# The head of a decoder layer on one Trainium2 core: halved first loads, products ahead of the token sums, ten idle products

## The reference

```
xn   = rms_norm(h) * g
proj = xn @ w_in        # query/key-value latents, rope key, recurrence input and gate, branch gates
attn = MLA(...)         # 8 heads, latent attention, causal
rec  = RG-LRU(...)      # causal conv of 4, gates a and i, linear recurrence, gelu gate
                        # a = exp(-8 * sigmoid(...) * softplus(-rg_lambda))
h = h + (sigmoid(g_a) * attn + sigmoid(g_r) * rec) @ w_out
h = h + MoE(rms_norm(h))   # 32 experts, top 4 of each token, clamped SwiGLU
out = rms_norm(h)[meta tokens dropped]
```

## Time and profile before

| | |
|---|---|
| median of 3 runs | 1166.68 us (1165.93 to 1167.15) |
| profiled execution, its own time | 1166.7 us |
| its span | 1164.9 us |
| TensorE busy | 1130.6 us (97%) |
| VectorE, ScalarE busy | 229.1 us, 189.3 us |
| granted TensorE clock, mean | 0.996 |
| HBM read | 440.53 MB |

### The profile page before, as it was taken

How to read it: one execution, slowest core, us unless ns; L and a number is a source line. 1 busy time by engine, 2 the same in 40 slices (tenths; PEclk the granted TensorE clock), 3 DMA queues, 4 the chain that set the end, 5 groups by cost and what they waited for, 6 DMA issues and landing times.

```text
span 1164.9 us, 13326 instructions
## 1 busy us (share of the span) xinstructions
PE 1130.6 (97%) x5608; PEld 524.5 (45%) x5608; DVE 229.1 (20%) x538; ACT 189.3 (16%) x412; POOL 0.2 (0%) x4
## 2 busy tenths in 40 slices
PE   8999999999999999999999999999999989999987
PEld 7778888844333333434343333333333333333422
DVE  5557510223011111111111111111111111111112
ACT  2466610022011010101011110101010101010102
POOL 0000000000000000000000000000000000000000
PEclk9999999999999999999999999999999999999999
DMA  9944436558999999999999999999999999999996
GB/s 374 396 152 174 159 150 248 224 203 333 416 431 430 430 428 437 433 430 433 432 433 432 432 433 432 433 432 434 432 432 433 433 433 433 432 426 428 430 425 271
DMA packets 30598, 442.14 MB, mean 380 GB/s; under 512 B 4640, under 2 KB 5152, under 8 KB 8160
## 3 DMA queue, kind: packets, MB, share of 16 engines
q1 hardware_dynamic: 27792, 438.93, 89.3%
q10 hardware_dynamic: 2768, 2.67, 0.7%
HBM read 440.53 MB, written 1.05 MB: 379 GB/s over the span
## 4 chain that ended last, share of the span: by engine, by line
PE 85%; DMA 13%; ACT 1%; another core or an unknown queue 0%; issue 0%; DVE 0%; SPq 0%; DVEq 0%; ACTq 0%
PE ps L941 33%; PE ps L960 16%; PE ps L577 11%; DMA work<-in_w_exp_dram 8%; PE ps L928 5%; PE ps L916 5%; DMA ring<-in_w_exp_dram 4%; PE ps L798 2%; PE ps L865 2%; PE ps L887 2%; PE ps L822 1%; ACT work L1405 1%; PE ps L950 1%; PE ps L922 1%; PE ps L661 1%; PE ps L614 1%
## 5 line engine op out<-in xcount | busy, mean ns | idle before, releaser
L941 PE MATMUL ps<-ring,work 128*64 128x512 f32 x1536 | 344.3, 600 | 11.7 <-DMA ring<-in_w_exp_dram 11.7
L941 PEld LDWEIGHTS ps<-ring,work 128*64 128x64 f32 x1536 | 109.9, 138 | 230.3 <-issue 219.0
L1857 DVE TENSOR_SCALAR work<-ps 128x512 f32<-128x512 f32 x32 | 22.1, 692 | 724.9 <-PE ps L941 724.9
L577 PE MATMUL ps<-work,ring 128*128 128x256 f32 (+1 forms) x560 | 125.9, 384 | 0.0
L941 PE MATMUL ps<-work 128*64 128x512 f32 x512 | 115.8, 596 | 1.9 <-DMA work<-in_w_exp_dram 1.9
L960 PE MATMUL ps<-ring,work 128*64 128x512 f32 x512 | 113.8, 596 | 3.9 <-ACT work L1405 3.8
L960 PE MATMUL ps<-work 128*64 128x512 f32 x504 | 112.5, 596 | 4.4 <-ACT work L1405 3.8
L577 PEld LDWEIGHTS ps<-work,ring 128*128 128x128 f32 x560 | 105.4, 190 | 17.1 <-issue 0.9
L941 PEld LDWEIGHTS ps<-work 128*64 128x64 f32 x512 | 35.3, 137 | 77.8 <-issue 73.6
L960 PEld LDWEIGHTS ps<-ring,work 128*64 128x64 f32 x512 | 35.3, 137 | 71.9 <-issue 63.0
L928 PE MATMUL ps<-work 64*128 64x512 f32 x256 | 67.5, 627 | 0.0
(11 more groups left out here) (261 smaller groups left out, 612.8 us busy)
## 6 DMA issues: line engine op xcount, KB each, us to landing
ring<-in_w_exp_dram SPq DMA_DIRECT2D x40, 4096.0 KB, 42.2
work<-in_w_exp_dram SPq DMA_DIRECT2D x20, 4096.0 KB, 42.1
ring<-in_w_exp_dram SPq DMA_DIRECT2D x38, 2048.0 KB, 18.3
work<-in_w_exp_dram SPq DMA_DIRECT2D x19, 2048.0 KB, 17.3
ring<-in_w_mix_dram SPq DMA_DIRECT2D x29, 1024.0 KB, 7.4
ring<-in_w_exp_dram SPq DMA_DIRECT2D x20, 1024.0 KB, 7.7
work<-in_w_exp_dram SPq DMA_DIRECT2D x9, 1024.0 KB, 11.9
ring<-in_w_mix_dram SPq DMA_DIRECT2D x2, 576.0 KB, 18.5
```

The source lines that it names most:

```text
L577: ins = nc.tensor.matmul(ps[part:part + width, b, 0:hi - lo], wv[:, k, o:o + width], rows[:, k, lo:hi], start=(k == 0), stop=(k == KT - 1))
L941: ins = nc.tensor.matmul(ps[CAP * c:CAP * c + CAP, b, :], xeT[:, k, CAP * (u % 2):CAP * (u % 2) + CAP], wu[:, k % SPAN, 512 * q:512 * q + ...
L1857: V.tensor_scalar(hg, ps[:, 0, :], LIMIT, None, ALU.min).then_inc(glu_ready, 1)
```

## The change

SyncE issues `vec` (all the small vectors, 101 floats a partition) first and then slot 0 in two halves, which are its blocks 0 to 3 and 4 to 7, each with a semaphore of its own (`head_in`); the later loads follow unchanged. ScalarE issues x in two halves instead of two quarters; SyncE issues none of x. All four squares are at ScalarE. The first products begin with the first halves; the token sums stand in front of block 6; the long idle product is gone, and there are ten short ones for nine. On VectorE the first two softplus instructions go ahead of `xw`, the long chain behind the squares of `cq`. On ScalarE the Exp comes first and the Sqrt table is loaded behind the squares.

```diff
-MIX_LANDINGS = [len(range(s, M0, SLOTS)) for s in range(SLOTS)]
+MIX_LANDINGS = [len(range(s, M0, SLOTS)) - (s == 0) for s in range(SLOTS)]
...
-            for c in (0, 2):
-                spe.dma_start(xT[:, 2 * c:2 * c + 2, :], xT_in[:, 2 * c:2 * c + 2, :]).then_inc(xT_in_s[c], 16)
             spe.dma_start(vec[:, :], vec_in[:, :]).then_inc(vec_in_s, 16)
+            for c in range(2):
+                q = SLOT // 2
+                spe.dma_start(ring[:, 0, q * c:q * c + q], w_mix[0, :, q * c:q * c + q]).then_inc(head_in[c], 16)
             for n, (kind, a, w) in enumerate(LOADS):
                 s = n % SLOTS
+                if n == 0:
+                    continue
...
-            keep_clock(0, 9)
+            keep_clock(0, 10)
...
-            keep_clock_long(2, xsq[:, 0, :], 1)
-            wait_load(load_at[("in", 0)])
+            def token_sums():
+                for k in range(KT):
+                    if k % 2 == 0:
+                        pe.wait_ge(xsq_act, k // 2 + 1)
...
             wv = wslot(load_at[("in", 0)], KT)
             for k in range(KT):
+                if k == 6:
+                    token_sums()
+                if k % 4 == 0:
+                    pe.wait_ge(head_in[k // 4], 16)
                 pe.wait_ge(xw_ready, k + 1)
...
-            for c in (1, 3):
-                act.dma_start(xT[:, 2 * c:2 * c + 2, :], xT_in[:, 2 * c:2 * c + 2, :]).then_inc(xT_in_s[c], 16)
+            for c in range(2):
+                act.dma_start(xT[:, 4 * c:4 * c + 4, :], xT_in[:, 4 * c:4 * c + 4, :]).then_inc(xT_in_s[c], 16)
             act.wait_ge(consts_set, 1)
-            nc.scalar.activation(dummy, dummy, ACT.Sqrt)
-            for c in (0, 2):
-                act.wait_ge(xT_in_s[c], 16)
+            nc.scalar.activation(dummy[:, 0:1], dummy[:, 0:1], ACT.Exp)
+            act.wait_ge(softplus_in, 1)
+            nc.scalar.activation(sp[:, 0:8], sp[:, 0:8], ACT.Exp, scale=-1.0).then_inc(sp_exp, 1)
+            for c in range(4):
+                if c % 2 == 0:
+                    act.wait_ge(xT_in_s[c // 2], 16)
                 nc.scalar.activation(xsq[:, 2 * c:2 * c + 2, :], xT[:, 2 * c:2 * c + 2, :], ACT.Square).then_inc(xsq_act, 1)
             act.dma_start(ca[:, P:], ca_in[:, P:]).then_inc(const_in, 16)
+            nc.scalar.activation(dummy[:, 1:2], dummy[:, 1:2], ACT.Sqrt)
             act.wait_ge(xsum_done, 1)
...
```

More of the change, by code:

```diff
@@ L348, in layer @@
             sem(n) for n in ("const_in", "vec_in_s", "x_in_s"))
-        xT_in_s = [sem(f"xT_in{c}") for c in range(4)]
+        xT_in_s = [sem(f"xT_in{c}") for c in range(2)]
+        head_in = [sem(f"head_in{c}") for c in range(2)]
         moe_in, bdn_in, gfin_in = (
@@ L589, in keep_clock @@
                     nc.tensor.matmul(ps[:, bank, 0:P], ones, ones, start=True, stop=True)
[L591 to L594 removed]
             pe.wait_ge(consts_set, 1)
[L597 removed]
+            keep_clock(0, 10)
             Q = T // 4
[L599 to L605, removed]
[L606 to L609 removed]
+            def token_sums():
+                for k in range(KT):
+                    if k % 2 == 0:
+                        pe.wait_ge(xsq_act, k // 2 + 1)
+                    for q in range(4):
+                        ins = nc.tensor.matmul(ps[32 * q:32 * q + 32, 7, 0:Q], ones[:, 0:32], xsq[:, k, Q * q:Q * q + Q],
+                                               start=(k == 0), stop=(k == KT - 1))
+                ins.then_inc(xsum_done, 1)
             wv = wslot(load_at[("in", 0)], KT)
             for k in range(KT):
+                if k == 6:
+                    token_sums()
+                if k % 4 == 0:
+                    pe.wait_ge(head_in[k // 4], 16)
                 pe.wait_ge(xw_ready, k + 1)
@@ L1527, in _ @@
                 ins = V.memset(spread[32 * q:32 * q + 1, :], 1.0)
[L1528 to L1531, removed]
             dve.wait_ge(vec_in_s, 16)
-            for c in (0, 2):
-                dve.wait_ge(xT_in_s[c], 16)
+            lam = vec[:, VEC_AT["rg_lambda"]:VEC_AT["rg_lambda"] + 8]
+            link(V.tensor_scalar(sp[:, 8:16], lam, -1.0, None, ALU.mult))
+            V.tensor_tensor(sp[:, 0:8], sp[:, 8:16], lam, ALU.max).then_inc(softplus_in, 1)
             for k in range(KT):
+                if k % 4 == 0:
+                    dve.wait_ge(xT_in_s[k // 4], 16)
                 V.tensor_scalar(xw[:, k, :], xT[:, k, :], v("norm_mix_g", k), None, ALU.mult).then_inc(xw_ready, 1)
-            dve.wait_ge(xstd_done, 1)
-            V.reciprocal(rx_std, rx_std).then_inc(rstd_ready, 1)
-            lam = vec[:, VEC_AT["rg_lambda"]:VEC_AT["rg_lambda"] + 8]
             V.tensor_scalar(hba, vec[:, VEC_AT["b_rg_a"]:VEC_AT["b_rg_a"] + 8], 0.5, None, ALU.mult)
@@ L1542, in _ @@
             V.tensor_scalar(hbg, vec[:, VEC_AT["b_gate"]:VEC_AT["b_gate"] + 16], 0.5, None, ALU.mult)
-            link(V.tensor_scalar(sp[:, 8:16], lam, -1.0, None, ALU.mult))
-            V.tensor_tensor(sp[:, 0:8], sp[:, 8:16], lam, ALU.max).then_inc(softplus_in, 1)
+            dve.wait_ge(xstd_done, 1)
+            V.reciprocal(rx_std, rx_std).then_inc(rstd_ready, 1)
+            dve.wait_ge(rstd_done, 1)
+            dve.wait_ge(xw_ready, KT)
+            rstd = ps[:, 3:7, 0:T // 4]
+            for k in range(KT):
+                V.tensor_tensor(xnT[:, k, :].rearrange("p (q t) -> p q t", q=4),
+                                xw[:, k, :].rearrange("p (q t) -> p q t", q=4), rstd, ALU.mult).then_inc(xn_ready, 1)
+            ex = eps_x.rearrange("p (q t) -> p q t", q=4)
+            V.reciprocal(ex, rstd)
+            dve.wait_ge(xn_ready, KT)
+            V.memset(rxp[:, :, 0:CONV - 1], 0.0).then_inc(xs_read, 1)
+            link(V.memset(ckvm.rearrange("p k v c j -> p (k v c j)"), 0.0))
+            dve.wait_ge(proj_read, JOB[("cq", QT - 1)] + 1)
+            link(V.tensor_tensor(sqq, cq, cq, ALU.mult))
+            link(V.tensor_tensor(sqq[:, 0, :], sqq[:, 0, :], sqq[:, 1, :], ALU.add))
+            V.tensor_tensor(sqq[:, 0, :], sqq[:, 0, :], sqq[:, 2, :], ALU.add).then_inc(lora_sq, 1)
             dve.wait_ge(sp_exp, 1)
@@ L1561, in _ @@
             V.tensor_scalar(nhc, sp[:, 24:32], LRU_C / 2, None, ALU.mult).then_inc(hc_ready, 1)
[L1564 to L1579, removed]
             dve.wait_ge(proj_read, JOB[("ckv", KVT - 1)] + 1)
```

10 lines of the change are left out of this document (4 added, 6 removed).

## The result

| | before | changed |
|---|---|---|
| median (9 runs each) | 1167.01 us | 1169.31 us |
| single times | 1165.93 to 1169.33 us | 1168.84 to 1170.81 us |
| profiled execution, its own time | 1166.7 us | 1169.28 us |
| its span | 1164.9 us | 1167.5 us |

The ratio is 1.0022, 95% interval 1.0013 to 1.0031: the changed kernel is slower by some 2.5 us. One execution of it took 2993 us; it is neither in the ratio nor in the single times above. The forecast was 1165.3 us, range 1164.0 to 1166.9.

The account below looks back on a forecast made before the run. TensorE, then the weight stream it releases, was taken to bound the kernel. First product 6.65 + sixteen products 7.11 + token sums 1.2 = 14.96 us against 16.34, so 1166.7 - 1.4 = 1165.3 us, range 1164.0 to 1166.9.

Parts of the forecast that it names:

- rival D: Head: slower if the first product starts after 8.03 us, slot 0's first half landing hardly before the second; 1167.9 us, chance 0.06.
- Rival E: First products: TensorE's clock at 1.2 GHz makes eight products cost 3.6 us more; 1168.9 us, chance 0.05.
- F: Start of TensorE's first product in the head, set by the weights' landing: 6.65 us, bounds 5.9 and 7.2.
- from then I use 0.408 MB per us: Head loads: DMA rate assumed after 5.00 us, by when 1.005 MB had moved, to turn bytes into landing times.
- the lag from the last byte to the landing: Head loads: a landing is seen some 0.2 MB (0.45 us) after its share of bytes.
- the head start I gave to SyncE's queue: Head loads: about half of vec gone before x's packets, slot 0's first half complete after 1.47 to 1.5 MB, not 1.69.
- strict turns of packets: Head loads: if the two queues alternate strictly by packet, slot 0's first half is seen at 7.2 us.
- The gap and the clock: TensorE's wait between tenth idle product and first product: 0.9 us, leaving the clock up, at no cost.
- S, the token sums: Token sums, now in line between twelfth and thirteenth product: add 1.2 us, between 0.9 and 1.4.
- Second halves, ScalarE, softplus chain, table load: Rest of head: second halves covered by 1 us, squares and table by 1.1; moved softplus chain and dropped table load worth nothing.
- One to one to the end: From head to kernel end: TensorE releases the loads, so the head's 1.4 us gain reaches the end whole.

Follow-up runs that it names:

- e9: Changed kernel with all mixer loads at a row pitch of 8320 bytes in HBM instead of 8192, half rows kept: 1169.72 us, one execution.
- e4: Changed kernel with the two halves of slot 0 each laid out in one piece in HBM: 1167.71 us, ratio 1.0003.
- e6: e4 with 19 idle products instead of ten: 1165.95 us, ratio 0.9991.
- e5: Kernel before with slot 0 in two halves, each in one piece in HBM: 1165.63 us, ratio 0.9987.
- e10: e4 with ScalarE loading only x's first half; SyncE loads vec, slot 0's first half, x's second, slot 0's second: 1165.24 us, ratio 0.9984.
- e8: e4 with all head loads on SyncE's queue: vec, x's first half, slot 0's first, x's second, slot 0's second: 1166.28 us, ratio 0.9989.
- e2: Kernel before with only slot 0 loaded in two halves, first products waiting for half each: 1167.06 us, ratio 0.9999.
- e7: Changed kernel with slot 0 in one transfer again, first products waiting for all of it: 1169.03 us, one execution.
- e3: Changed kernel with vec issued behind slot 0's first half instead of ahead of it: 1169.58 us, ratio 1.0019.

## Why the prediction was wrong

The arithmetic that I gave to rival D decided: the token sums are in line, and the first product came after 8.03 us. D's reason did not: the first half landed 1.4 us before the second (1.2 + 7.4 and 1.6 + 8.4 us). Rival E came on top. Neither was my forecast; that E's 1168.9 us lies near the measured time is luck, since E left F where it was. By the steps:

- *F, the first product*: failed. 6.65 forecast, 7.2 my upper bound, 8.61 measured. By the packets of the trace it parts into three. The first miss is the rate: "from then I use 0.408 MB per us". The half rows brought it to 264 GB/s, and the last packet of the first half ended at 7.46 us; at another pitch (e9) it ended at 6.67, with contiguous halves at 6.64 and 6.61 (e4, e6). So 0.8 us are the pitch's. My 0.408 held only for transfers that had been seen in the trace, and a half row had not. The second is the lag from the last byte to the landing: 1.1 us in the changed kernel and in e4, 0.5 in e6 and e9, and I had taken 0.45 from x. That is 0.6 us which the pitch alone doesn't explain, since e4 has it too; in before slot 0 itself landed when 0.4 MB more had moved than lay ahead of it, and I should have taken the lag from that row. The third is the head start I gave to SyncE's queue: "slot 0's first half is some 3 packets of 8 per engine ahead". `vec` did go through first, but slot 0's rows started only at 3.83 us, when x's first half was nearly through. In e9, without the dip and with the short lag, the first product came at 7.21, so 0.56 us are that. That 7.21 is also my number for strict turns of packets owes something to luck: as many bytes lay ahead, but from 3 to 4 us there were no equal turns.
- *The gap and the clock*: failed, 1.68 us. "A gap of 0.9 us, and gaps of 0.48 and 1.45 left the pace alone" was right for these gaps; the real one was 2.88 us. I had priced this as rival E, at 3.6 us, and not tied it to F, though a late F is just what makes the gap. It cost less than half of that, because the clock was back at 1.00 from 12.5 us on.
- *S, the token sums*: right. 1.08 us and 0.20 for the change-over (5.38 + 1.93 against 7.11), forecast 1.2. In line they cost what I had put into rival D's break-even.
- *Second halves, ScalarE, softplus chain, table load*: right, all covered. x's second half was taken up at 9.07, not 8, and was still in time for a ninth product that was late itself.
- *One to one to the end*: right in the medians. 2.34 us at `spread`, 2.35 at 160 us, 2.6 in the span, 2.5 in the ratio; with the other sign, e5 has 1.13 us at `spread` and 1.5 in the ratio, e10 1.82 and 1.9. A single execution does not show it: against the span of before, e5 with its 1.13 us ended 0.1 us later, e8 with 1.58 only 0.2 us earlier, e10 with 1.82 2.6 us earlier. In e5 the lead was whole at 597 us, so it is the late part, where the weight stream ends the kernel, that differs.

The sum with what was measured: 8.61 + 7.06 + 1.08 + 1.93 = 18.68. Against 14.96 that is 1.96 (F), 1.68 (clock) and 0.08 (sums with change-over).

The Trainium skill's advice against cutting a transfer in two partition halves ("DMA: Bandwidth & Descriptors", section "Rules for kernel authors") I had taken as no hindrance to column halves. Here the column halves did no better than the advice says of partition halves: the cut gained nothing in e2, and in the changed kernel nothing against e7's whole slot (8.61 and 8.55 us). The first product came earlier only where the half rows were contiguous or at another pitch.

On the cause, the same page of the Trainium skill, section "Latency and other measured facts", states that in copies of 16 KiB per partition, row pitches at large powers of two, from 512 KiB on, lose bandwidth, and that 4 KiB of padding restored it while 192 bytes did not. Here a pitch of 8 KiB lost it already when half of each row was read, and 128 bytes of padding restored it (264 to 410 GB/s from 5 to 7 us).

Open: why a pitch of 8192 and half rows collide, and why a landing was seen 0.5 us after its last byte in some executions and 1.1 in others. In e2 from 8 to 9 us packets of the same kind moved at 426 GB/s again, and in the changed kernel at 452; that the engines were by then no longer all in the same half is a guess that no run tested. Whether the clock falls at a gap of about 2.2 us seems to differ between executions (e4: 1165.72 to 1170.23 us), which no second trace shows; why is open too.

## What to carry to other kernels

Halve a load of this shape only if each half is one piece in HBM, or with another pitch (one execution here); read the GB/s of the stretch afterwards, not the count of bytes. When work that filled a wait is moved in line, the wait must shrink by more than that work, and its own worst case must be priced together with the clock: a late operand costs once as a wait and once more as slow products behind the gap. Put what the first product needs in one order on few queues, and read from the trace when its first row starts: with the short rows of `vec` in front, the weights started at 3.83 us while the other queue had the engines.

## What the runs showed of the hardware

- Two DMA queues that both have rows waiting move about equal numbers of rows, not of bytes: 33 and 35 packets with 0.27 and 0.14 MB in before, 36 and 38 packets in the changed kernel from 6 to 7 us. A load behind 128 short rows can start late all the same: with `vec` in front slot 0's first row started at 3.83 us, with `vec` behind it (e3) at 1.75.
- A half row of 4096 bytes at a pitch of 8192 took 0.32 us per engine (e2, 6 to 7 us), as long as a whole row of 8192 in before's stretch: 63.8% of 16 engines for 33 packets is 0.31 us. Two microseconds later such rows moved at 426 GB/s.
- The same transfer in the same layout was seen to land 0.5 us after its last packet in one execution (e6) and 1.1 us after it in another (e4).
- The granted clock fell after 2.88, 2.92, 2.96 and 2.18 us without products (changed kernel, e3, e7, e4), not after 1.51 us or less where it had risen before. Ten idle products are on the edge of its rise: it rose at 4.76 us in e3, at 6.45 in e8, and in e9 not before 13.4 us, which cost 3.06 us.
